# Windowed attention on TensorE: two 64-feature heads issued in one step, in the halves of the array

## The reference, cut to what matters

```
logits = (q @ k.T) * scale + bias          # 128 queries x 128, 256 or 384 keys
m = maximum(logits.max(-1), sink)
p = exp(logits - m)
o = (p @ v) / (p.sum(-1) + exp(sink - m))
```

## Time and profile before

| | us |
|---|---|
| median of 3 runs | 2811.51 (2810.06 to 2822.33) |
| the profiled execution's own time | 2829.72 |
| its span | 2827.9 |
| PE busy | 2403.5 (85%) |
| DVE busy | 1694.9 (60%) |
| ACT busy | 880.5 (31%) |
| POOL busy | 857.4 (30%) |

### The profile page before, as it was taken

How to read it: one execution, slowest core, us unless ns; L and a number is a source line. 1 busy time by engine, 2 the same in 40 slices (tenths; PEclk the granted TensorE clock), 3 DMA queues, 4 the chain that set the end, 5 groups by cost and what they waited for, 6 DMA issues and landing times. The chain is left out here.

```text
span 2827.9 us, 34169 instructions
## 1 busy us (share of the span) xinstructions
PE 2403.5 (85%) x12190; PEld 1496.6 (53%) x12190; DVE 1694.9 (60%) x3944; ACT 880.5 (31%) x1983; POOL 857.4 (30%) x649
## 2 busy tenths in 40 slices
PE   8998999988997788777777777776989999798888
PEld 7886566875552344332222223222767887655766
DVE  7997655546776777766776677664036334334362
ACT  3224443143232342322322233222243222233331
POOL 0003111445543355433333344332322222200133
PEclk9999999999999998999999999999988999859899
DMA  4332001439999999999999999997212222302142
GB/s 148 108 104 93 36 34 67 153 128 400 421 421 420 421 420 417 415 421 421 419 408 421 415 414 410 418 415 306 94 56 77 72 85 69 108 34 75 57 171 82
DMA packets 131078, 682.53 MB, mean 241 GB/s; under 512 B 13536, under 2 KB 23136, under 8 KB 65120
## 3 DMA queue, kind: packets, MB, share of 16 engines
q0 software_dynamic: 73728, 536.90, 45.9%
q1 hardware_dynamic: 57184, 143.47, 14.3%
HBM read 655.68 MB, written 24.64 MB: 241 GB/s over the span
## 5 line engine op out<-in xcount | busy, mean ns | idle before, releaser
L1678 PE MATMUL bank<-peer_uv,peer_diag 128*128 128x512 f32 x2048 | 968.1, 618 | 291.5 <-ACT peer_diag L1337 279.4
L1571 DVE SCALAR_TENSOR_TENSOR peer_uv<-peer_uv,early_h 128x1024 f32<-128x1024 f32 x512 | 645.8, 1272 | 383.3 <-DMA peer_uv<-in_peer_uv,peer_index 379.9
L1678 PEld LDWEIGHTS bank<-peer_uv,peer_diag 128*128 128x128 f32 x2048 | 384.3, 196 | 835.4 <-issue 830.8
L1372 POOL DMA_INDIRECT peer_uv<-in_peer_uv,peer_index x512 | 529.0, 1033 | 747.9 <-PE bank L1678 658.2
L223 POOL TENSOR_TENSOR weight_low<-weight_ring,weight_high 128x1024 fp32r<-128x1024 f32 x102 | 247.9, 2431 | 919.3 <-ACT weight_high L206 919.3
L155 PE MATMUL bank<-hT_high,weight_high 128*128 128x512 f32 x952 | 414.2, 435 | 22.0 <-POOL weight_low L223 7.3
L157 PE MATMUL bank<-hT_high,weight_low 128*128 128x512 f32 x952 | 381.9, 401 | 0.0
L156 PE MATMUL bank<-hT_low,weight_high 128*128 128x512 f32 x952 | 381.6, 401 | 0.0
L206 ACT ACTIVATE weight_high<-weight_ring 128x1024 fp32r<-128x1024 f32 x171 | 180.8, 1057 | 513.7 <-PE bank L157 489.1
L1332 ACT ACTIVATE peer_gelu<-peer_dots 128x2 f32<-128x2 f32 x256 | 52.0, 203 | 791.0 <-DVE peer_uv L1571 790.8
L155 PEld LDWEIGHTS bank<-hT_high,weight_high 128*128 128x128 f32 x952 | 184.8, 194 | 83.4 <-issue 35.2
(11 more groups left out here) (414 smaller groups left out, 2969.1 us busy)
## 6 DMA issues: line engine op xcount, KB each, us to landing
weight_ring<-in_weights SPq DMA_DIRECT2D x171, 512.0 KB, 3.2
z_store<-fill_stage SPq DMA_DIRECT2D x70, 256.0 KB, 2.4
peer_uv<-in_peer_uv,peer_index POOLq DMA_INDIRECT x512
merge_z<-z_store SPq DMA_DIRECT2D x8, 768.0 KB, 6.3
merge_z<-z_store SPq DMA_DIRECT2D x12, 512.0 KB, 4.7
score_store<-peer_work SPq DMA_DIRECT2D x16, 192.0 KB
peer_sc<-score_store SPq DMA_DIRECT2D x24, 128.0 KB
swz<-z_store SPq DMA_DIRECT2D x1, 2560.0 KB, 9.8
```

The lines of the kernel that those rows point to most:

```text
L1372: pool.indirect_dma_start(uv[:, p % SLOTS], None, peer_uv, bass.IndirectOffsetOnAxis(index[:, n % 2, p % TOPK:p % TOPK + 1], 0)).then_inc( ...
L1571: nc.vector.scalar_tensor_tensor(uv[:, p % SLOTS, 0:D], uv[:, p % SLOTS, 0:D], 1.0, h2[:, t], ALU.mult, ALU.mult, accum_out=dots[:, p % TO ...
L1678: mm = nc.tensor.matmul(bank[2 * (t % 2) + c][:], diag[:, p % SLOTS], uv[:, p % SLOTS, D + c * 512:D + (c + 1) * 512], start=(p % PICKS == ...
```

## The change

Where a head has 64 features (`per` = 2: attn1 and attn2), a step takes units 2j and 2j + 1 together. TensorE's step j is then: scores of both heads, one filler step, values of the pair j - 3, turn of the pair j - 2, another filler step. Values alternate between the two heads over the key blocks. VectorE does the maxima of pair j interleaved with the divisors of pair j - 1; ScalarE copies the turned pair j - 2 and then does the exponentials of pair j. The numbers of banks and buffers stay as they are. Where a head has 128 features (attn3) the order of every engine stays as it is. With 35 steps of two filler portions attn1 has 70 places for the filler, where it had 69; attn2 has 38, where it had 37.

```diff
--- before.py
+++ after.py
@@ -384,6 +384,8 @@
     n = len(units)
     width = max(u["k"].shape[-1] for u in units)
     per = P // dim
+    steps, side_by_side = n // per, lambda j: range(per * j, per * j + per)
+    turn_after, keep_after, values_after, divide_after = (3, 4, 5, 2) if per == 1 else (2, 2, 3, 1)
     with Stage(nc, name) as st:
         logit = st.sb("logit", [P, B, width])
         prob = st.sb("prob", [P, B, width])
@@ -425,26 +427,33 @@
                                               diag[:, i % B], start=True, stop=True)
                     mm.then_inc(turned, 1)
 
-                def values(i):
-                    u, g = units[i], i // group
-                    pe.wait_ge(turned_kept, i + 1)
+                def values(beside):
+
+                    g, last = beside[0] // group, len(units[beside[0]]["v"]) - 1
+                    pe.wait_ge(turned_kept, beside[-1] + 1)
                     if g >= 2:
                         pe.wait_ge(out_kept, g - 1)
-                    at = u["half"] * dim
-                    col = (i % group) // per * P
-                    for c, v in enumerate(u["v"]):
-                        mm = nc.tensor.matmul(bank[4 + g % 2][at:at + dim, col:col + P], v,
-                                              probT[:, i % 2, c * P:(c + 1) * P], start=(c == 0),
-                                              stop=(c == len(u["v"]) - 1))
-                    mm.then_inc(out_ready, 1)
-
-                for i in range(n + 5):
-                    if i < n:
-                        scores(i)
-                    if 3 <= i < n + 3:
-                        turn(i - 3)
-                    if i >= 5:
-                        values(i - 5)
+                    for c in range(last + 1):
+                        for i in beside:
+                            at, col = units[i]["half"] * dim, (i % group) // per * P
+                            mm = nc.tensor.matmul(bank[4 + g % 2][at:at + dim, col:col + P], units[i]["v"][c],
+                                                  probT[:, i % 2, c * P:(c + 1) * P], start=(c == 0), stop=(c == last))
+                            if c == last:
+                                mm.then_inc(out_ready, 1)
+
+                for j in range(steps + values_after):
+                    if j < steps:
+                        for i in side_by_side(j):
+                            scores(i)
+                    if per == 2:
+                        fill.pe(pe, fill_steps)
+                    if j >= values_after and per == 2:
+                        values(side_by_side(j - values_after))
+                    if turn_after <= j < steps + turn_after:
+                        for i in side_by_side(j - turn_after):
+                            turn(i)
+                    if j >= values_after and per == 1:
+                        values(side_by_side(j - values_after))
                     fill.pe(pe, fill_steps)
                     fill.mark()
 
@@ -505,14 +514,15 @@
                         dve.wait_ge(high_kept, g + 1)
                         nc.vector.tensor_tensor(out_low(g).bitcast(F32R), src, out(g), ALU.subtract).then_inc(out_kept, 1)
 
-                for i in range(n + 6):
-                    rows = [maximum(i)] if i < n else []
-                    if 2 <= i < n + 2:
-                        rows.append(divisor(i - 2))
+                for j in range(steps + values_after + 1):
+                    rows = [maximum(i) for i in side_by_side(j)] if j < steps else []
+                    if divide_after <= j < steps + divide_after:
+                        rows += [divisor(i) for i in side_by_side(j - divide_after)]
                     for _ in zip_longest(*rows):
                         pass
-                    if i >= 6 and (i - 6) % group == group - 1:
-                        keep((i - 6) // group)
+                    done = per * (j - values_after)
+                    if done > 0 and done % group == 0:
+                        keep(done // group - 1)
 
             @block.scalar
             def _(act):
@@ -537,13 +547,15 @@
                         act.wait_ge(out_ready, i - 1)
                     nc.scalar.activation(probT[:, i % 2, 0:k], bank[2 + i % 2][:, 0:k], ACT.Copy).then_inc(turned_kept, 1)
 
-                for i in range(n + 4):
-                    if i >= 4:
-                        keep(i - 4)
-                    if i < n:
-                        exps(i)
-                    if i:
-                        fill.act(act, fill.marks[i - 1])
+                for j in range(steps + keep_after):
+                    if j >= keep_after:
+                        for i in side_by_side(j - keep_after):
+                            keep(i)
+                    if j < steps:
+                        for i in side_by_side(j):
+                            exps(i)
+                    if j:
+                        fill.act(act, fill.marks[j - 1])
                 fill.act(act)
 
             @block.sync
```

## The result

The changed kernel takes 2716.16 us (median of 4 runs, 2712.59 to 2718.61), the kernel before beside it 2810.78 us (median of 4, 2806.2 to 2822.33): a ratio of 0.9641, 95% interval 0.9606 to 0.9676, 94.6 us less. The forecast was 2714 in a range of 2698 to 2756. The profiled executions lie further apart, 2829.72 and 2718.61 us, 111 us; where those 17 us went is the first thing that the experiments settle.

The account below looks back on a forecast made before the run. TensorE was taken to bound attn1 and attn2, about 320 of 2828 us. Savings of 56 us in attn1 and 45 in attn2 make 101: 2811.5 - 101 + 4 = 2714 us, range 2698 to 2756.

Parts of the forecast that it names:

- One head's time for two in scores and values: TensorE, per pair: two heads run side by side, scores 0.84 or 0.62 us, values 0.80 or 0.58.
- from 0.43 for four: TensorE's turn: 4 matmuls take 0.43 us, each further one 0.11, so 12 take 1.31 and 8 take 0.87.
- What is late next: VectorE and ScalarE fit, 2.6 us slack before turn; 3 us more waiting in attn1's ramp and tail, 56 us less.
- attn2 and its clock: attn2 starts at 1.2 GHz and rises after about 15 us, costing 7: 73 us instead of 118.4, 45 less.
- The row from another place: Outside attn2, under matmuls following each other without change of shape, the clock rose within 4.8 us.
- I give 4 us for that: Allowance in the sum: the profile ran 18 us above the median; attn2 may have woken earlier in timed runs.
- (a): attn2's clock stays low or rises as late as before, only 1 to 15 us gained there: 2740 to 2755; chance 0.12.
- (b): Strict program order of matmuls in scores and values costs 17 us in attn1, 6 in attn2: 2737; 0.10 shared by three rivals.
- (c): Scores' row halves don't overlap at all, values as forecast, 23 us lost: 2737; chance 0.10 shared by three rivals.
- (f): Nothing runs side by side, only shape changes saved, 37 us less: 2775; chance 0.03 together with other small effects.
- (d): VectorE's handover becomes the bound, TensorE waits up to 2 us in some 11 units: 2736; 0.10 shared by three rivals.
- (e): Ramp waits let attn1's clock fall and attn2's old behaviour repeats, up to 2858 us; chance 0.03.

Follow-up runs that it names:

- both scores in the same rows: Changed kernel with both heads' scores reading partitions 0 to 63, so no row halves side by side: 2739.84 us, ratio 0.972 to the kernel before.
- the scores apart: Changed kernel with the second head's scores behind the first filler step instead of beside the first head's: 2752.04 us, ratio 0.977 to the kernel before.
- the kernel entered at the higher clock: Kernel before plus 32 matmuls of constants on TensorE in the idle time ahead of attn2: 2816.14 us, ratio 0.9989.
- the filler in twos: Kernel before, one head per step, with two filler steps behind every second unit instead of one behind each: 2799.13 us, ratio 0.9942.
- head-by-head values: Changed kernel with a pair's values issued as the whole first head, then the whole second, not alternating: 2721.44 us, ratio 0.9651 to the kernel before.

## Why the prediction was right

**The terms.** One head's time for two in scores and values: 0.84 and 0.80 us measured with 384 keys, as forecast. Turn in one run: 1.36 (forecast 1.31). The pair: 4.78 and 3.90 us against 4.73 and 3.84. The step that was slightly off is "from 0.43 for four": that row stems from the ramp, and in the steady step turn takes 0.04 to 0.05 us more. With the other terms' hundredths a pair is 0.05 or 0.06 us longer, 1.8 us over 16 pairs each.

Where attn1's 59.9 us come from, by the runs: 16.9 for the scores' overlap, 16.8 for the values', 3.1 for idle time. The remaining 23 us fit 32 pairs with four changes of shape less each, at the 0.19 us that moving one of them showed: 24 us, an estimate. No run takes both overlaps away at once, so that these parts add up isn't shown.

**What is late next.** The forecast allowed 3 us more waiting in ramp and tail. There was less than before: TensorE stood idle for 1.1 of 140.0 us, before for 4.2 of 199.9. By the single records a diagonal was ready 1.3 to 1.8 us ahead of its turn in most of the old steps, but only 0.1 us at every eighth unit, behind a held operation, where some of TensorE's waits of 0.8 us lie; in pairs with the full pipeline and a held operation, 1.4 us or more remained. So the slack covers VectorE's held operations, which the old order's did not. Hence attn1's 59.9 us instead of 56. The pairing did not only shorten TensorE's row, its two-step distance is looser in time than the old three single steps.

**attn2 and its clock.** 15 us at 1.2 GHz were forecast, 5.6 were measured, with 5.7 in two further profiles. The stage took 65.8 us, not 73: 5 us of the difference are the clock, and TensorE stood idle for 1.0 us, not 3. The reason that the prediction gave, fewer changes of shape and both row halves in use, is not what the runs show. With both scores in the same rows the clock rose after 9.0 us as well, and with the scores apart, which start with the same small pieces as the old order (two score matmuls, three of the filler, with the same starts for the first 7 us), after 9.2. All eight rises of the paired orders came in the ramp, ahead of the stage's first turn, so the steady pair can't be their cause.

What sets the orders apart in the profiles is the first wait for a diagonal. The old order meets it 4 to 8 us into attn2, as here in the first profile:

```profile
2488.41 0.77 PE L424 MATMUL bank<-attn_diag,attn_prob 128*128 128x128 f32 x2 [0.62 <-DVE attn_diag L495]
```

Where the clock was already up there, it fell: at the end of the wait of 1.64 us in the kernel entered at the higher clock, in the 1.90 us of the kernel with pairs in attn1 alone, and behind the 2.91 us of the filler in twos, early in which it had risen. Where it was still low, with waits of 0.62 us, it stayed low until 12.7, 38.9 and 69.6 us from the stage's start. In the paired orders TensorE's first long wait in attn2 (0.71 to 1.00 us, in one profile none) came after the rise, and none in either stage was longer than 1.00. In the same two stages no wait of up to 1.50 us at the higher clock was followed by a fall. This is a correlation over 14 profiles, most orders with one each; no run takes the wait away and leaves the rest, and what exactly raises the clock stays open. The row from another place that the prediction compared with the earlier trace rows also leaves out what came ahead of it: TensorE had been busy at 0.50 for 6.98 us with matmuls of one column, so the 4.8 us aren't the whole time to that rise.

**The sum.** The step that was mis-sized is the allowance "I give 4 us for that". Against the profiled execution the gain was 111 us, not 101; against the median it was 94.6, because the profile shown had 69.6 us of attn2 at the lower clock, and the timed runs around the median have a higher mean clock than its 0.950: 17 us, not 4. The two errors, 10 us too little gain and 13 too little allowance, nearly cancel, and 2714 against 2716.16 is closer than the working deserved. Of the 10 us, 4 come from attn1's waits and 7 to 8 from attn2, less 1.4 for all the rest; the allowance is attn2's clock alone.

**The rivals.** (a) did not occur in any of eight profiles with pairs in attn2 (5.5 to 9.2 us at 0.50). (b) is refuted in its strict form by the changed kernel's own row (x4 in 0.92 us) and by head-by-head values; a weaker form, a lead of three matmuls, exists and costs nothing in the changed order. (c) and (f) are refuted by the two kernels that take one overlap away, each 17 us slower in attn1. (d): no wait of that kind. (e) did not occur, attn1 ran at 1.00 in all 14 profiles; but a ramp did lose the clock in attn2 under the old order, with single waits of 1.64 and 1.90 us, so that the danger it names exists.

The Trainium skill's rule of strict order (TensorE: Matmul & The Clock Gate, "Part 3: Packing small matmuls — row/col tiling") does not agree with the records here: the second head's chain starts at 360.408 us, ahead of the first one's fourth matmul at 360.511. Its statement that tiles of other rows or columns run concurrently does agree: x4 in 0.92 us, x12 in 0.88.

## What to carry to other kernels

Products that fill half of the array's rows or columns are worth pairing across heads when TensorE sets the stage's time: the partner costs only its issue. Alternate the partners in portions of at most four matmuls (with four nothing was lost here, with six 0.28 us a pair), and count the changes of array shape in a step (0.2 us each here), since a piece moved to stand beside one of its own shape saves one. Look at the waits in a stage's ramp, and not only at its steady step: here they stood where the clock was lost. Before trusting a single profile of a stage that starts after an idle gap, profile the same kernel again: its clock may be chance, and a change that makes the clock's rise dependable narrows the spread and lowers the median.

## What the runs showed of the hardware that was not expected

The granted clock of one and the same stage differed between executions of one program: 69.6, 12.7 and (with attn1 changed) 66.0 us at 1.2 GHz under an identical sequence of steps, worth up to 23 us of 2810. The clock once up, single waits of 1.64 and 1.90 us went with its fall, where waits of up to 1.50 us did not. And a steady stream of matmuls without a gap (34.07 of 34.10 us busy) can stay at 1.2 GHz, while the same step holds 2.4 GHz once it is there.

One half of the array overtook three matmuls issued ahead of it for the other half, and no more: a second head whose six matmuls were issued behind the first head's six started right behind the first head's third. And a change between 64x128, 128x64 and 128x128 pieces cost 0.19 to 0.22 us at 2.4 GHz.
